# FFN of a decoder trunk: nine of eleven chunks in seven products, and another order of the FFN's end

## The reference

```python
def rmsnorm(x, g):
    y = x32 * lax.rsqrt(jnp.mean(x32 * x32, axis=-1, keepdims=True) + EPS)
    return (y * g).astype(x.dtype)

def swiglu(x, wg, wu, wd):          # wg, wu: 1024 x 2816, wd: 2816 x 1024
    return (jax.nn.silu(x @ wg) * (x @ wu)) @ wd

for i in range(DEPTH):
    x = x + 0.5 * rmsnorm(swiglu(rmsnorm(x, g[0]), ffn1_wg[i], ffn1_wu[i], ffn1_wd[i]), g[1])
    x = x + rmsnorm(mixer(rmsnorm(x, g[2])), g[3])
    x = x + 0.5 * rmsnorm(swiglu(rmsnorm(x, g[4]), ffn2_wg[i], ffn2_wu[i], ffn2_wd[i]), g[5])
```

## Time and profile before

| | |
|---|---|
| median of 3 executions | 1986.74 us (1986.46 to 1988.91) |
| profiled execution, device time | 1986.53 us |
| its span in the trace | 1984.7 us, with 1.8 us around it |
| PE busy | 1976.4 us (100%), 14806 matmuls |
| DVE busy | 1572.3 us (79%) |
| ACT busy | 1089.7 us (55%) |
| transfers | 386.37 MB, mean 195 GB/s |

### The profile page before, as it was taken

One profiled execution on the slowest core, in us unless ns is written; L12 is line 12 of the kernel. 1 busy time (PEld: TensorE's weight loads), 2 busy tenths in 40 slices (PEclk: granted clock), 3 DMA queues, 4 the chain that ended last, 5 costly groups with the idle time before them and its releaser, 6 DMA issues.

```text
span 1984.7 us, 36138 instructions
## 1 busy us (share of the span) xinstructions
PE 1976.4 (100%) x14806; PEld 1844.0 (93%) x14806; DVE 1572.3 (79%) x1783; ACT 1089.7 (55%) x1208; POOL 26.5 (1%) x52
## 2 busy tenths in 40 slices
PE   9999999999999999999999999999999999999998
PEld 8999989998999999988998999998999899998998
DVE  8987678878887877768887887657887888677885
ACT  6555445555555665666555555645555555545553
POOL 0000000000000000000000000000000000000000
PEclk9999999999999999999999999999999999999999
DMA  7654645554554644435555555634555555654552
GB/s 264 243 213 179 250 170 191 194 217 183 212 212 171 236 169 153 167 128 191 212 191 213 190 194 217 238 137 149 212 191 212 191 202 202 232 193 159 212 192 105
DMA packets 56291, 386.37 MB, mean 195 GB/s; under 512 B 6752, under 2 KB 7136, under 8 KB 11232
## 3 DMA queue, kind: packets, MB, share of 16 engines
q1 hardware_dynamic: 52416, 372.07, 50.8%
q10 hardware_dynamic: 3744, 12.39, 1.9%
HBM read 383.39 MB, written 1.05 MB: 194 GB/s over the span
## 4 chain that ended last, share of the span: by engine, by line
PE 98%; DVE 1%; DMA 1%; issue 0%; ACT 0%; POOL 0%; DVEq 0%; POOLq 0%; SPq 0%
PE ps L553 22%; PE ps L554 22%; PE ps L555 22%; PE ps L559 6%; PE ps L561 6%; PE ps L560 6%; PE ps L575 2%; PE ps L578 2%; PE ps L572 2%; PE ps L715 1%; PE ps L712 1%; PE ps L711 1%; PE ps L594 1%; PE ps L923 0%; PE ps L685 0%
## 5 line engine op out<-in xcount | busy, mean ns | idle before, releaser
L1615 DVE TENSOR_TENSOR w_low<-raw,w_high 128x2048 fp32r<-128x2048 f32 x287 | 650.3, 2286 | 93.9 <-ACT w_high L1165 93.9
L553 PE MATMUL ps<-xT_both,w_high 128*128 128x256 f32 x2304 | 638.6, 277 | 0.0
L554 PE MATMUL ps<-xT_both,w_high 128*128 128x256 f32 x2304 | 637.4, 277 | 0.0
L555 PE MATMUL ps<-xT_both,w_low 128*128 128x256 f32 x2304 | 637.0, 276 | 0.0
L1165 ACT ACTIVATE w_high<-raw 128x2048 fp32r<-128x2048 f32 x287 | 546.1, 1911 | 46.2 <-DMA raw<-stream 36.6
L554 PEld LDWEIGHTS ps<-xT_both,w_high 128*128 128x128 f32 x2304 | 433.3, 188 | 0.0
L555 PEld LDWEIGHTS ps<-xT_both,w_low 128*128 128x128 f32 x2304 | 432.7, 188 | 0.0
L553 PEld LDWEIGHTS ps<-xT_both,w_high 128*128 128x128 f32 x2304 | 432.6, 188 | 0.0
L1209 ACT ACTIVATE region<-ps 128x256 f32<-128x256 f32 x176 | 67.1, 382 | 454.0 <-PE ps L555 444.1
L559 PE MATMUL ps<-xT_both,w_high 128*128 128x256 f32 x736 | 207.6, 282 | 0.3 <-ACT xn L1281 0.3
L561 PE MATMUL ps<-xT_both,w_high 128*128 128x256 f32 x736 | 205.0, 278 | 0.0
(11 more groups left out here) (220 smaller groups left out, 3004.7 us busy)
## 6 DMA issues: line engine op xcount, KB each, us to landing
raw<-stream SPq DMA_DIRECT2D x351, 1024.0 KB, 4.8
gain<-gains ACTq DMA_DIRECT2D x23, 512.0 KB, 5.3
x<-x_in SPq DMA_DIRECT2D x2, 512.0 KB, 4.5
raw<-stream SPq DMA_DIRECT2D x2, 512.0 KB, 6.5
region<-rope_in SPq DMA_DIRECT2D x1, 512.0 KB, 5.7
out<-x SPq DMA_DIRECT2D x1, 512.0 KB, 2.6
att_mask<-att_mask_in SPq DMA_DIRECT2D x1, 320.0 KB, 5.7
out<-x SPq DMA_DIRECT2D x1, 256.0 KB, 2.0
```

What stands on the lines that cost most here:

```text
L553: nc.tensor.matmul(acc, lh, rh, start=start, stop=False, skip_group_check=goes_on)
L554: nc.tensor.matmul(acc, lh, rl, start=False, stop=False, skip_group_check=goes_on)
L555: return nc.tensor.matmul(acc, ll, rh, start=False, stop=stop, skip_group_check=goes_on)
L1615: nc.vector.tensor_tensor(w_low[:, p % RING, :], raw[:, p % RAW, :], w_high[:, p % RING, :], ALU.subtract).then_inc(piece_split, 1)
```

## The change

Nine chunks (0 to 8) instead of eight are done in seven products; chunks 9 and 10 stay plain. Of chunk 8's seven products, five are done in its unit: those for banks 1, 5, 2 behind block 18 (`LAST_FIRST`) and 3, 4 behind block 19 (`LAST_SECOND`). Those for banks 7 and 6 are needed for tile 1's y only. They stand behind tile 0's last chunk (`LAST_DEFERRED`), and the two additions of `join` that touch banks 6 and 7 are cut off as `join_second`. Banks 0 and 1 alternate for the last two blocks only. Tile 0's order is now chunk 9 for both halves, then chunk 10 for both. Tile 0's normalized x is made in two instructions of 512 columns, and behind an FFN the transposes of its first half stand in front of the last three matmuls, those of its second half in front of the last one. The lows and highs of the next sublayer's pieces 2 and 3 move from the joint to the FFN's end, with low(3) cut in two halves that stay in the joint, behind `gain_y` of y's first half and behind `update_x`. Two places in the mixers do the first product behind transposes with its first matmul cut in two (`products_at_entry`).

```diff
-SEVENS = 8
+SEVENS = 9
-FIRST_SUM_BANK = SEVEN[SEVEN_SPLIT][0]
+LAST_FIRST, LAST_SECOND, LAST_DEFERRED = (0, 4, 5), (6, 3), (1, 2)
 def gu_bank(i):
-    return GU_BANK + (i % 2 if i < EARLY or i >= BLOCKS - 4 else 0)
+    return GU_BANK + (i % 2 if i < EARLY or i >= BLOCKS - 2 else 0)
...
+            def products_at_entry(acc, lh, ll, rh, rl, start, stop):
+
+                for part in range(2):
+                    some = slice(part * P, (part + 1) * P)
+                    nc.tensor.matmul(acc[:, some], lh, rh[:, some], start=start and part == 0, stop=False)
+                nc.tensor.matmul(acc, ll, rh, start=False, stop=False)
+                return nc.tensor.matmul(acc, lh, rl, start=False, stop=stop)
...
                 def unit(c, turn=0):
 
+                    parts = (range(SEVEN_SPLIT), range(SEVEN_SPLIT, len(SEVEN)))
+                    first, second = parts if c < SEVENS - 1 else (LAST_FIRST, LAST_SECOND)
                     block(2 * c + 2, w0 + block_piece(2 * c + 2), turn)
-                    seven(c, 0, SEVEN_SPLIT, turn)
+                    seven(c, first, turn)
                     block(2 * c + 3, w0 + block_piece(2 * c + 3), turn)
-                    seven(c, SEVEN_SPLIT, len(SEVEN), turn)
+                    seven(c, second, turn).then_inc(piece_used, 1)
...
-                for i in range(BLOCKS - 4, BLOCKS):
+                for i in range(BLOCKS - 2, BLOCKS):
                     block(i, w0 + block_piece(i))
...
+                        ends = c == CHUNKS - 1 and j == FT - 1
+                        if ends and t == 1 and half == 1:
+                            transpose_next(sub, (0,))
+                            acc = ps[:, Y_BANK + 3, :]
+                            for rh in (w_high, w_low):
+                                nc.tensor.matmul(acc, oT_hi[:, at, tok], rh[:, p % RING, cols], start=False, stop=False,
+                                                 skip_group_check=True)
+                            transpose_next(sub, (1,))
+                            return nc.tensor.matmul(acc, oT_lo[:, at, tok], w_high[:, p % RING, cols], start=False, stop=True,
+                                                    skip_group_check=True)
...
+                pe.wait_ge(joined, 7 * ffn_no(sub) + 5)
+                for c in range(CHUNKS - 2, CHUNKS):
+                    pe.wait_ge(hT_split, s0 + splits_up_to(FT * c + 1))
+                    weights_ready(w0 + down_piece(c))
                     for half in range(2):
+                        last = chunk(c, 0, half)
+                        if c == CHUNKS - 1:
+                            last.then_inc(y_ready, 1)
+                pe.wait_ge(joined, 7 * ffn_no(sub) + 7)
+                seven(SEVENS - 1, LAST_DEFERRED)
+                chunk(CHUNKS - 2, 1, 0)
+                chunk(CHUNKS - 1, 1, 0).then_inc(y_ready, 1)
+                chunk(CHUNKS - 2, 1, 1).then_inc(piece_used, 1)
+                chunk(CHUNKS - 1, 1, 1).then_inc(piece_used, 1)
...
                 if joint:
                     gain_y(joint, 0, 0)
                     if after_ffn(joint):
-                        low(w0 + 2)
+                        low_part(w0 + 3, 0)
                     gain_y(joint, 0, 1)
                     update_x(joint, 0)
+                    if after_ffn(joint):
+                        low_part(w0 + 3, 1)
...
                 times_up(sub, BLOCKS - 4)
                 low(w0 + 29)
-                h_low(sub, BLOCKS - 4)
                 low(w0 + 30)
+                low(w0 + 31)
                 times_up(sub, BLOCKS - 3)
-                low(w0 + 31)
-                h_low(sub, BLOCKS - 3)
+                low(w0 + 32)
+                join(sub)
+                low(w0 + FFN_PIECES)
                 times_up(sub, BLOCKS - 2)
-                low(w0 + 32)
+                chunk_low(sub, SEVENS)
                 h_low(sub, BLOCKS - 2)
+                low(w0 + FFN_PIECES + 1)
                 times_up(sub, BLOCKS - 1)
+                join_second(sub, 0)
                 h_low(sub, BLOCKS - 1)
-                low(w0 + FFN_PIECES)
-                low(w0 + FFN_PIECES + 1)
+                join_second(sub, 1)
+                low(w0 + FFN_PIECES + 2)
```

200 lines of the change are left out of this document (96 added, 104 removed).

## The result

| | before | with the change |
|---|---|---|
| median device time | 1987.76 us, 10 runs (1986.15 to 1989.04) | 1992.84 us, 10 runs (1990.13 to 1993.45) |
| ratio | | 1.0024 (95%: 1.0016 to 1.0032) |
| profiled execution | 1986.53 us, span 1984.7 | 1992.30 us, span 1989.9 |

The change makes the kernel 5.1 us slower, 0.24%, with an interval that lies wholly above 1. The prediction had said 1984.8 and a range up to 1988.2, and had given a result over 0.2% slower a chance of 0.11. In spans the two profiled executions are 5.2 us apart, in device time 5.8: between span and device time lie 1.8 us before and 2.4 with the change (1.8 to 1.9 in all 75 further runs of the kernel before, 2.3 or 2.4 in six of the ten runs of the change).

What follows compares the result with a forecast made beforehand. PE (TensorE) was taken as the bound, busy 1976.4 of 1984.7 us. Terms -5.04 + 3.15 - 0.30 + 0.06 + 0.30 = -1.83 us gave 1984.8 us, range 1981.3 to 1988.2.

Steps and rivals of the forecast that it cites:

- The matmuls: Chunk 8 in seven products: 0.63 us less PE time per FFN, 5.04 us over eight.
- The mechanism at the FFN's end: In seven FFNs PE waits for the 512-column normalized x, DVE gapless from low(32) to `gain_y`, high(32) released by DMA.
- 7 x 0.45 = 3.15: PE's wait before the transposes, 0.45 us in each of seven FFNs, loses 3.15 of the 5.04 us gained.
- the working: DVE's chain laid on the old kernel's clock at one FFN's end: transposes can start at 455.18.
- done by 448.2: At the FFN's end, the square of y's first half is ready before DVE is free at 448.41.
- Costs nothing to 0.1, and is contained in the 0.44: Wait at tile 0's last chunk for `h_low(21)`: 0 to 0.1 us, contained in the transposes' wait.
- the forecast 0.44: PE's wait at an FFN's transposes: ready at 455.18 against 454.74 on PE's own path.
- Attention, start-up, cuts: Small edits: attention wait gone, -0.30 us; start-up x in two, +0.06; three split first matmuls, 0 to 0.3, taken as +0.30.
- The halves of x: Tile 0's x in two instructions keeps the FFN-end wait from being 0.6 us larger.
- Chunk 8's cover: Chunk 8's first part would not wait for chunk 7's sums: ready at 422.2, PE comes at 423.38, 1.2 us cover.
- PE's own path is at its issue rate: PE's matmul path cannot run faster, so a gain beyond closing the 0.44 us wait is excluded.
- C: Rival, slower: piece 32's fetch takes 6.11 us, not 4.8, so 1.75 us wait per FFN, 1993.8 us; chance 0.11.

Runs made afterwards that it cites:

- g1: Changed kernel with low(34) cut in two, join's second and third additions swapped, and low(3)'s halves behind `update_x` of either tile: 1987.38 us, ratio 0.9997.
- g2: g1 plus the first matmul cut in two at the first weights-stationary product in both convolutions and attention: 1986.86 us, ratio 0.9996.

## Why the prediction was wrong

*The matmuls.* -5.04 worked out for the FFNs and up to +0.30 for the small cuts; -5.13 in the nominal distances, and 0.13 for a cut where it was made alone (49.00 against 48.87 for a convolution's first stretch). Right.

*The mechanism at the FFN's end.* Right: seven waits for the 512-column normalization, no gap over 0.04 in DVE's queue from low(32) to `mean_first`, high(32) released by the DMA, and the eighth FFN keeps its gain (-0.60). Leaving work out of PE there moved nothing (12.1 us of waits), and taking load off DVE's chain gave back 5.5 us.

*Its size.* The term "7 x 0.45 = 3.15" is the first that failed: 7 x 0.86 = 6.0. The transposes stand at 457.64, and the working, moved by the 1.94 us of this trace, gives 457.12. Four places give 0.50 of the 0.52:

- Additions that read what the one right ahead wrote go 0.71 apart and not 0.60, twice: 0.23. I took 0.60 from the seven additions of before, where an addition always stands in between.
- Low(32) starts at 435.52 for 435.43: 0.09.
- The square of y's first half stands in ACT's queue behind high(36), which the DMA releases late, and ends 0.12 after DVE is free. I had held it done by 448.2 and had looked at DVE's queue only. ACT, and the end of the chain of waits with its two fetches:

```profile
448.30 1.92 ACT L1197 ACTIVATE w_high<-raw 128x2048 fp32r<-128x2048 f32 x1 [0.80 <-DMA raw<-stream]
450.13 0.57 ACT L1206 ACTIVATE xn<-ps 128x512 f32<-128x512 f32 x1
```

```profile
428.75 4.79 DMA raw<-stream
...
443.43 4.85 DMA raw<-stream
```

- PE follows the 512-column half by 0.81, not 0.75: 0.06.

The other 4.21 us from `mean_eps` to the normalization came out to the hundredth (452.62 to 456.83).

*"Costs nothing to 0.1, and is contained in the 0.44."* `h_low(21)` ends at 447.99, 0.35 later than worked out, by low(32) and the two additions. So the first matmul of tile 0's last chunk waits 0.16, and the second comes 0.34 behind it, 0.11 more than usual, for which I had no price: 0.27 and not 0.1. But it is contained, as was said. The chain of waits back from the transposes runs through POOL, DVE, ACT's high(36) and its fetch, and not through PE: time that PE loses here it would otherwise wait at the transposes. PE alone would be there at 454.74 + 1.94 = 456.68; the transposes come 0.96 later, which is the forecast 0.44 and the 0.52 above.

*Attention, start-up, cuts.* -0.50 for -0.30; +0.07 for +0.06 at the first transposes, though 0.2 more of waits stand behind them; 0.1 for each split: near enough. The prediction called 0.3 the longest wait of before after the start-up, but the list of that trace has one of 0.5 in the mLSTM layer (L1090, for DVE); it is 0.5 in the changed kernel too, so nothing hangs on it. *The halves of x* are worth 4.5 us of waits, against 0.6 x 7 = 4.2. *Chunk 8's cover* held.

*The term that wasn't there* is the second step that failed. The pace of the stream, which the prediction left out, gave up to +4.3 us in the profile, 2.4 of it in the convolutions. The prediction treated 0.113 us as the issue rate of PE ("PE's own path is at its issue rate"), though the trace of before has both paces. Behind the second entry of its convolution, near 245, the same product goes at 0.118, and in the change, with the cut that I priced at 0.1, it goes at 0.113:

```profile
247.00:255.00 8.00, 8.00 (x70) 8.00 (x69) 7.27 (x13) 4.32 (x4) 0.00 (x0) 1.00 0.37 132
```

```profile
249.00:257.00 8.00, 8.00 (x73) 8.00 (x72) 7.27 (x14) 4.57 (x4) 0.00 (x0) 1.00 0.35 122
```

The first is the kernel before, the second the changed one. A question to the trace of before, why one stretch has 0.113 and the next 0.118, would have shown that there is a risk of a microsecond in each such stretch.

*The rivals.* It ended on C's side, but not by C: the fetch that counts took 4.79 us, not 6.11. The two fetches that started 2.2 and 4.4 us behind it did take longer (5.07 and 5.43), but the chain doesn't run through them. The wait of 0.86 and the pace did it together: 6.0 + 4.3 lost, 5.1 + 0.5 won. By these sums, which are those of one profile each, the time without the pace would be about 1988.5, no change that a measurement can tell, and with the pace and the forecast wait about 1990.0: either failed step alone leads out of the range.

*What stays open.* What in the chip makes a stream quick or slow. Why the change lost the quick pace at the first entry, which it doesn't touch in code: it enters it at another distance from its waits, but kernels with other distances (g1, with most of the waits taken out, among them) were slow as well. How the medians divide: the kernel before has one profile, of an execution 1.2 us under its median of 1987.76, and which paces the slower ones have isn't recorded. What the 0.5 us more outside the span are, in a third to four fifths of the runs of every changed kernel. And some 4 us between g2 (1986.9) and what its matmuls and attention's wait would allow (1988.0 - 4.8 - 0.5 = 1982.7): its profile has 1.3 of waits in one FFN, 0.1 to 0.6 in each other one, and 2.0 of pace in small pieces, whose cause I don't know.

## What to carry to other kernels

An instruction that stands between a producer and the answer of another engine may be free where it is: look what fills each round trip before moving it, since the two edits here that took a filler away came out 1.9 and 5.5 us slower. In a chain worked out from start-to-start distances, take the distance from a pair with the same dependence, go through the queue of every engine on it (ACT's too), and give a wait of PE its restart, unless a later wait contains it. And before a matmul stream is priced at one rate, look whether the trace has it at two; a microsecond won in one place can be lost in a stretch that the change doesn't touch.
